# Four mixers and eight gated feed-forward stages on one core: order and form of the last mixer's products, and four smaller edits

## What is computed

```python
# block 1: F0, A, F1, then F2, G, F3       block 2: H, C0, then N, C1
x = x + 0.5 * g * swiglu(modulate(rms_norm(x)), wg, wu, wd)       # F0..F3
x = x + g * mixer(modulate(rms_norm(x)))                         # A, G, H, N
x = x + g * conv_ffn(modulate(rms_norm(x)))                      # C0, C1
# G: z = gelu(h @ w_in); u, v = split(z); v = layer_norm(v)
#    out = (u * (w_s_causal @ v + b_s)) @ w_out
# N: q, k_c, v_c, k_s, v_s, k_w, v_w, gate = split(h @ w_in)       16 heads, 4 groups
#    three softmax branches (compressed, selected, window), each with a sloped
#    distance bias; out = (sigmoid(gate) weighted sum of the branches) @ w_out
```

## Time and profile before

| what | value |
|---|---|
| median of three runs | 1769.36 us (1767.43 to 1771.12) |
| the profiled execution | 1770.44 us, span 1768.8 us |
| mean granted TensorE clock | 0.995 |
| busy share of the span | PE 97%, DVE 80%, ACT 52%, POOL 24% |
| moved by DMA | 411 MB, 233 GB/s |

### The profile page before, as it was taken

The page is one execution under the profiler, slowest core; times in us unless marked ns, Lnnn a source line. Parts: engine busy times, 40 slices in busy tenths (PEclk is TensorE's granted clock), DMA queues, the critical chain, the costliest instruction groups (busy, mean ns, idle before and its releaser), DMA issues. The chain is left out here.

```text
span 1768.8 us, 36564 instructions
## 1 busy us (share of the span) xinstructions
PE 1723.2 (97%) x14077; PEld 1679.1 (95%) x14077; DVE 1419.0 (80%) x1914; ACT 911.9 (52%) x1274; POOL 420.1 (24%) x685
## 2 busy tenths in 40 slices
PE   7999999999999999999999999899999999999998
PEld 6999999999999999989999998889999997799998
DVE  6767898788869878877977899869988996578555
ACT  3443367864345533466543366556444557664444
POOL 5322311013223223120122344421222123401000
PEclk9999999999999999999999999999999999999999
DMA  9998857548987888855698865335989593147550
GB/s 338 358 340 271 301 182 265 168 165 307 325 285 250 282 275 303 287 203 195 232 333 269 303 218 202 108 120 168 329 292 305 154 236 111 48 138 256 170 187 24
DMA packets 261793, 411.45 MB, mean 233 GB/s; under 512 B 21950, under 2 KB 204414, under 8 KB 261560
## 3 DMA queue, kind: packets, MB, share of 16 engines
q1 hardware_dynamic: 224968, 290.67, 50.0%
q0 software_dynamic: 36720, 119.36, 19.1%
HBM read 408.90 MB, written 2.63 MB: 233 GB/s over the span
## 5 line engine op out<-in xcount | busy, mean ns | idle before, releaser
L2786 DVE TENSOR_TENSOR lo<-raw,hi 128x2048 fp32r<-128x2048 f32 (+1 forms) x257 | 581.6, 2265 | 178.8 <-ACT hi L2613 178.5
L2613 ACT CAST hi<-raw 128x2048 fp32r<-128x2048 f32 (+1 forms) x266 | 499.0, 1879 | 385.6 <-PE dacc L2305 194.5
L2303 PE MATMUL up<-operand_hi,hi 128*128 128x256 f32 x1952 | 553.8, 284 | 2.4 <-DVE lo L2786 2.4
L2304 PE MATMUL up<-operand_lo,hi 128*128 128x256 f32 x1952 | 553.1, 283 | 0.0
L2305 PE MATMUL up<-operand_hi,lo 128*128 128x256 f32 x1952 | 553.0, 283 | 0.0
L2082 POOL DMA_DIRECT2D ada<-in_ada_w_dram x448 | 260.0, 597 | 816.8 <-DVE ada_acc L2822 753.4
L2303 PEld LDWEIGHTS up<-operand_hi,hi 128*128 128x128 f32 x1952 | 375.3, 192 | 3.3 <-DVE lo L2786 3.0
L2304 PEld LDWEIGHTS up<-operand_lo,hi 128*128 128x128 f32 x1952 | 375.4, 192 | 0.0
L2305 PEld LDWEIGHTS up<-operand_hi,lo 128*128 128x128 f32 x1952 | 375.4, 192 | 0.0
L2822 DVE SCALAR_TENSOR_TENSOR ada_acc<-ada,c_col,ada_acc 128x512 f32<-128x512 f32 x420 | 318.9, 759 | 13.1
L2303 PE MATMUL dacc<-act_hi,hi 128*128 128x256 f32 x1072 | 303.6, 283 | 2.6 <-DVE act_lo L2999 2.6
(11 more groups left out here) (459 smaller groups left out, 2734.6 us busy)
## 6 DMA issues: line engine op xcount, KB each, us to landing
ada<-in_ada_w_dram POOLq DMA_DIRECT2D x448, 256.0 KB, 4.6
raw<-in_ffn_wg_dram SPq DMA_DIRECT2D x88, 512.0 KB, 5.3
raw<-in_ffn_wu_dram SPq DMA_DIRECT2D x88, 512.0 KB, 5.1
raw<-in_ffn_wd_dram SPq DMA_DIRECT2D x88, 512.0 KB, 5.4
raw<-in_ffn_w_up_dram SPq DMA_DIRECT2D x88, 512.0 KB, 4.5
raw<-in_ffn_w_down_dram SPq DMA_DIRECT2D x46, 512.0 KB, 4.4
raw<-in_hg_w_in_dram SPq DMA_DIRECT2D x32, 512.0 KB, 4.9
raw<-in_attn_w_qkv_dram SPq DMA_DIRECT2D x24, 512.0 KB, 7.7
```

Of the source, the lines that this page charges most:

```text
L2303: pe.matmul(o, stat[0], mov[0], start=start, stop=False, skip_group_check=True)
L2304: pe.matmul(o, stat[0], mov[1], start=False, stop=False, skip_group_check=True)
L2613: last = act.copy(put(slab(hi, s, SPL)), take(slab(raw, s, RAW)))
L2786: last = dve.tensor_tensor(put(slab(lo, s, SPL)), take(slab(raw, s, RAW)), put(slab(hi, s, SPL)).bitcast(F32), ALU.subtract)
```

## The change

1. N, gates: slab b+8 is split over its 48 gate columns only and multiplied with these as stationary operand (24 matmuls of 256 columns, 48 x 256 out); ScalarE copies the rows, two small transposes bring them to positions x 48, then the sigmoid.
2. N, order: the gate transposes and scores(0) stand between the two halves of slab b+9, the turn of the compressed probabilities between the halves of b+10. ScalarE copies these before the second value slab. VectorE scales head 1 ahead of head 2's bias and minimum. GpSimd makes the bias of head n + 2 before it waits for head n's coefficients.
3. N, end: the splits of the output slabs b+11 to b+13 move behind the head loop on VectorE and to its last rounds or behind it on ScalarE (b+11 ahead of the loop); the idle products go; the output's first two banks no longer wait for the last results.
4. Vector 23 is now among F3's five; vector 18 is made in G (tiles between the splits, its sum behind the output). H makes none; its wait for the last left-over vector stands ahead of slab b+9.
5. G: the first value slab waits for each half of the scaled gate products separately, its loops are exchanged, and the first half is scaled ahead of the normed operand; slab b+8's low split is halved around the affine step, b+9's stands later.
6. F0: the first four tiles of vector 2 are loaded with the others behind the first slab's use instead of ahead of the bias table.
7. C0, C1: the first conv's bias step is chained on ScalarE instead of counted.

```diff
-FIRST_VEC = {"F0": 2, "A": 7, "F1": 8, "F2": 13, "F3": 18, "H": 23, "C0": 24, "C1": 29}
+FIRST_VEC = {"F0": 2, "A": 7, "F1": 8, "F2": 13, "G": 18, "F3": 19, "C0": 24, "C1": 29}
...
+            if s == BASE["N"] + 8:
+                gate_cols = lambda t: t.rearrange("p (k n) -> p k n", k=KB)[:, :, SEQ - 3 * NSA_HEADS:SEQ]
+                return [(gate_cols, gate_cols)]
...
             raw_products("G")
-            pe.wait_ge(S["up_scaled"], raw_first.index("G") + 1)
             for m in range(4):
                 slab_ready(b + 2 + m)
-                row_product(b + 2 + m, operand_stat(m), m == 0, m == 3, normed_count("G") - KB + 2 * m + 2)
+                row_product(b + 2 + m, operand_stat(m), m == 0, m == 3, normed_count("G") - KB + 2 * m + 2,
+                            first_of="G" if m == 0 else None)
                 if m == 2:
                     turn_weights()
             for m in range(2):
@@ -999,7 +1003,11 @@
                 if c >= 2:
                     pe.wait_ge(S["gelu_done"], 3 + c)
                 mix(c)
-            pe_out("G", pe, slab_ready, down_product, operand_mov)
+            for m in range(4):
+                slab_ready(b + 8 + m)
+                pe.wait_ge(S["operand_ready"], 4 * OPND["Go"] + m + 1)
+                down_product(b + 8 + m, operand_mov(m), m == 0, m == 3)
+            ada_sum(FIRST_VEC["G"])
...
             for m in (4, 5, 6, 7):
                 split_lo(b + m)
+                for k in {5: (0,), 6: (1,), 7: (2,)}.get(m, ()):
+                    ada_tile(FIRST_VEC["G"], k)
...
-            split_lo(b + 8)
+            split_lo_half(b + 8, 0)
             dve.wait_ge(S["bs_in"], 48)
             affine(0)
             affine(1)
-            split_lo(b + 9)
+            split_lo_half(b + 8, 1)
             gate(0)
             gate(1)
             gated_lo(0)
             gate(2)
             gated_lo(1)
+            split_lo(b + 9)
             gate(3)
             gated_lo(2)
             gated_lo(3)
             for m in (10, 11, 12):
                 split_lo(b + m)
+                for k in {10: (3,), 11: (4, 5), 12: (6, 7)}.get(m, ()):
+                    ada_tile(FIRST_VEC["G"], k)
             residual("G")
...
-                if c == 2:
-                    pe.wait_ge(S["mod_done"], 24)
...
+                if m == 9:
+                    pe.wait_ge(S["mod_done"], left_vector("H") + 1)
...
-            ada_sum(23, o=bank(up, 1))
...
-            ada_tile(23, 0)
-            ada_tile(23, 1)
...
-            ada_tile(23, 2)
...
-                if m < 14:
-                    ada_tile(23, m - 6)
...
             for n in range(NSA_HEADS):
+                if n + 2 < NSA_HEADS:
+                    nsa_pool_bias(pool, n + 2)
                 pool.wait_ge(S["ncoef"], n + 1)
                 early = n_prob[n % 3][:, 512:768].rearrange("p (r k) -> p r k", r=2)
                 c = n_coef[:, 4 * (n % 3):4 * (n % 3) + 2]
                 pool.tensor_tensor(early, early, c.unsqueeze(2).to_broadcast([P, 2, P]),
                                    ALU.mult).then_inc(S["nearly_scaled"], 1)
-                if n + 2 < NSA_HEADS:
-                    nsa_pool_bias(pool, n + 2)
...
+            def gate_columns(m):
+
+                w = 3 * NSA_HEADS
+                slab_ready(b + m)
+                for k in range(KB):
+                    o = (k + 1) * SEQ - w
+                    dst, stat = bank(dacc, 0)[0:w, 0:SEQ], [slab(t, b + m, SPL)[:, o:o + w] for t in (hi, lo)]
+                    pe.matmul(dst, stat[0], op_k(operand_hi, k), start=(k == 0), stop=False, skip_group_check=True)
+                    pe.matmul(dst, stat[0], op_k(operand_lo, k), start=False, stop=False, skip_group_check=True)
+                    last = pe.matmul(dst, stat[1], op_k(operand_hi, k), start=False, stop=(k == KB - 1), skip_group_check=True)
+                last.then_inc(slab_used, 1)
+
+            def turn_gates():
+
+                w = 3 * NSA_HEADS
+                pe.wait_ge(S["ngate_done"], 1)
+                for t in range(NT):
+                    last = pe.transpose(bank(dacc, 0)[:, SEQ + t * w:SEQ + (t + 1) * w], gate_rows[0:w, t * P:(t + 1) * P],
+                                        ident[0:w, 0:w])
+                last.then_inc(S["ngate_pe"], 1)
...
-            tokens(8, bank(dacc, 0), SEQ - 3 * NSA_HEADS, 3 * NSA_HEADS)
-            pe.wait_ge(S["nlo_done"], 6)
-            scores(0)
-            tokens(9, bank(dacc, 3), 0, SEQ)
+            gate_columns(8)
+            def gates_and_scores():
+                turn_gates()
+                pe.wait_ge(S["nlo_done"], 6)
+                scores(0)
+
+            tokens(9, bank(dacc, 3), 0, SEQ, gates_and_scores)
             pe.wait_ge(S["cl_done"], 1)
             scores(1)
-            tokens(10, bank(dacc, 2), 0, SEQ)
-            turn_compressed()
+            tokens(10, bank(dacc, 2), 0, SEQ, turn_compressed)
             for n in range(2, NSA_HEADS + 3):
                 if n < NSA_HEADS:
                     scores(n)
                 if n < NSA_HEADS + 2:
                     turn_probs(n - 2)
-                else:
-                    pe.wait_ge(S["nb_done"], NSA_HEADS)
-                    keep_warm(bank(up, 0), WARM)
                 if n == 3:
                     pe.wait_ge(S["nv_done"], 2)
                 if n >= 3:
                     values(n - 3)
 
-            pe.wait_ge(S["no_done"], NSA_HEADS // 2)
-            pe_out("N", pe, slab_ready, down_product, operand_mov)
+            def out_bank(q):
+
+                if q >= 2:
+                    pe.wait_ge(S["no_done"], NSA_HEADS // 2 - 3 + q)
+
+            for m in range(4):
+                slab_ready(b + 11 + m)
+                pe.wait_ge(S["operand_ready"], 4 * OPND["No"] + m + 1)
+                down_product(b + 11 + m, operand_mov(m), m == 0, m == 3, bank_free=out_bank if m == 0 else None)
...
-            split_hi(b + 10)
             act.wait_ge(S["kc_pe"], 2)
...
-            act.activation(gates, bank(dacc, 0)[:, 0:NT * 3 * NSA_HEADS], ACT.Sigmoid).then_inc(S["ngate_done"], 1)
-            split_hi(b + 11)
+            act.copy(gate_rows[0:3 * NSA_HEADS, :], bank(dacc, 0)[0:3 * NSA_HEADS, 0:SEQ]).then_inc(S["ngate_done"], 1)
+            split_hi(b + 10)
+            act.wait_ge(S["ngate_pe"], 1)
+            act.activation(gates, bank(dacc, 0)[:, SEQ:SEQ + NT * 3 * NSA_HEADS], ACT.Sigmoid).then_inc(S["ngate_done"], 1)
...
             exps(0)
             act.wait_ge(slab_used, b + 10)
             act.copy(vs_sb, bank(dacc, 3)).then_inc(S["nv_done"], 1)
-            split_hi(b + 12)
+            split_hi(b + 11)
             exps(1)
-            act.wait_ge(slab_used, b + 11)
-            act.copy(vw_sb, bank(dacc, 2)).then_inc(S["nv_done"], 1)
-            split_hi(b + 13)
             act.wait_ge(S["npt_pe"], 1)
             for j in range(2):
                 last = act.copy(c_pt[:, j * 512:(j + 1) * 512], bank(dacc, j))
             last.then_inc(S["npt_done"], 1)
+            act.wait_ge(slab_used, b + 11)
+            act.copy(vw_sb, bank(dacc, 2)).then_inc(S["nv_done"], 1)
             for n in range(2, NSA_HEADS + 3):
                 if n < NSA_HEADS + 2:
                     probs_back(n - 2)
                 if n < NSA_HEADS:
                     exps(n)
+                if n == NSA_HEADS + 2:
+                    split_hi(b + 12)
                 if n % 2 == 0 and n >= 4:
                     result(n - 3)
+            split_hi(b + 13)
             split_hi(b + 14)
...
             key_rest(1)
+            split_lo(b + 10)
             for n in range(NSA_HEADS + 1):
+                if n == 2:
+                    scale(1)
                 if n < NSA_HEADS:
                     bias_and_max(n)
                 if n == 0:
-                    split_lo(b + 10)
                     compressed_probs()
-                if n:
+                elif n != 2:
                     scale(n - 1)
-                if n in (0, 1, 3):
-                    split_lo(b + (11, 12, 0, 13)[n])
                 if n >= 8 and n % 4 == 0:
                     operand_rest(n // 4 - 2)
+            split_lo(b + 11)
+            split_lo(b + 12)
             operand_rest(3)
+            split_lo(b + 13)
             split_lo(b + 14)
...
-            for k in range(ATILES):
-                ada_load(pool, FIRST_VEC[phases[0]], k)
...
+                        if p == phases[0]:
+                            pool.wait_ge(slab_used, 1)
+                        for k in range(0 if p == phases[0] else ATILES, KB):
...
+                    for k in range(ATILES, KB):
+                        ada_load(pool, FIRST_VEC[p], k)
...
-                    for kk, t in [(kk, t) for kk in range(2) for t in range(NT)]:
+                    for t, kk in itertools.product(range(NT), range(2)):
+                        if first_of is not None and part == 0 and kk == 0:
```

(21 more changed lines are left out.)

27 lines of the change are left out of this document (11 added, 16 removed).

## The result

The changed kernel takes 1751.25 us (median of 4 runs, 1751.16 to 1752.15) against 1768.61 us (1767.43 to 1771.12): a ratio of 0.9899, interval 0.9887 to 0.9912, so 17.4 us less. The forecast was 1752.0 us. Another series, on another chip, gave 1752.53 us and 0.9908 (0.9895 to 0.9920).

What follows compares the result with a forecast made beforehand. TensorE, busy 97% of the span, was taken as the bound. N 13.6 + H 1.7 + F0 2.6 - G 0.3 = 17.6 us off 1770.44 gives 1752.8; with the median 1.1 lower, forecast 1752.0 us, range 1747 to 1762.

Steps and rivals of the forecast that it cites:

- N, gate slab and clock: N, slab 8 and behind: 24 wide matmuls replace 48 narrow ones, 3.5 us less; no low clock behind, 1.7 less.
- 5.9/48 = 0.123 us per matmul: N, slab 8: a full slab's time per matmul, pricing the 24 new matmuls at 2.95 us, 3.5 us less.
- N, stalls: N, entry to the head loop: waits on the compressed probabilities' copy (2.0) and VectorE's third scaling (1.8) go; 4.0 us.
- N, loop: N, head loop: bias one head ahead makes TensorE the bound; four pairs save 1.0 us, five heads behind as much; 2.0 us.
- N, end: N, end of head loop: eight idle products (1.98 us) and the output slabs' wait for the last result (0.46) go; 2.4 us.
- G: Gating mixer G: takes the modulation vector's tiles; its reordering's gain is lost again as VectorE has no idle time; costs 0.3 us.
- H: Hgrn mixer H: without the vector's tile ahead of the low-part splits, differences and TensorE's wait behind them come 1.7 us earlier.
- F0: Start phase F0: second slab's cast 0.9 us earlier and, as the gap halves, the clock's 1.7 us; 2.6 us.
- (1): N and F0: the clock still falls, giving back 3.4 + 1.7 us: 1757 us; chance 0.15.
- (2): N's tail becomes a wait: one slab late (4.2 us), the loop's 2.0 and F0 gain lost: 1761 us; chance 0.10.
- (3): N's loop turns wait on another engine, stalls only move; no loop, stall or F0 gain: 1760 to 1766 us; chance 0.10.
- (4): N, head loop: clock falls inside it and stays, making the kernel slower; whole loop low gives 1798 us; chance 0.03.

Runs made afterwards that it cites:

- Experiment 1: Changed kernel with slab 8's gate columns multiplied as before (48 matmuls streaming 48 columns, no two small transposes; split still over 384 columns): 1757.18 us.
- experiment 7: Changed kernel with the transposes of the compressed probabilities behind slab 10 again instead of between its halves: 1753.34 us.
- experiment 8: Changed kernel with the splits of output slabs 11 to 13 in the head loop again (ScalarE's casts of 12 and 13 ahead of it): 1755.16 us.
- experiment 2: Changed kernel with GpSimd making the bias of head n+2 behind the early product of head n again: 1753.59 us.
- experiments 3 and 4: Changed kernel with the eight idle products put back, between the value products of heads 14 and 15 (1755.79 us) or behind those of head 15 (1754.23 us).
- all_together: Changed kernel with alternating value products for heads 0 to 11, one G tile earlier, head 3's first scores and N's second hidden group later: 1746.42 us.

## Why the prediction was right

The time (1752.0 against 1751.25 and 1752.53), the sign and the stages were right, some of the terms only in their sum. The last step of the sum is rounded (1752.8 less 1.1 is 1751.7). By the two profiles the gain was 19.3 us where the sum had 17.6; that the medians meet so closely is in part the draw of the clock. The signs named in the forecast came: slab 8 in 2.82 us with no low clock behind it, no wait above 0.3 us ahead of the turns, a pair in 6.64 us, the first level product's wait down to 0.36 us, F0's second slab at 45.60 us.

- **N, gate slab and clock: 3.5 + 1.7 forecast, 5.25 measured.** Slab 8's start to the scores of head 2 took 22.27 us and takes 17.02. The sum is right, the split is not: the step "5.9/48 = 0.123 us per matmul" was good for the wide product, but I set it against 6.5 us that held 1.1 us of low clock. The product gives 2.6 less 0.3 for the transposes (my low end was 2.4), the clock the other 3.0, which is what 6.8 us at 0.213 instead of 0.120 us per product cost. Experiment 1 shows the first and brings back one of the two stretches.
- **N, stalls: 4.0 forecast, 4.26 measured** (scores of head 2 to those of head 6, 16.24 to 11.98 us). The causes were weighed wrongly. I gave the compressed turn's place 2.0 us; it is worth 0.76 (experiment 7). The splits were worth over 3 (experiment 8): VectorE's stand ahead of two scalings, as I had it, and what I missed is that ScalarE's cast and copy of a slab also stood ahead of its copies of the compressed probabilities.
- **N, loop: 2.0 forecast, 1.67 measured** from head 6 to the last pair, 1.74 by experiment 2. A pair at 6.64 and four at 26.54 us are the forecast's numbers (6.64, 26.56). Only "the five heads behind hold about as much" was too high.
- **N, end: 2.4 forecast, 3.26 measured** (1536.64 to 1542.67 before, 1520.61 to 1523.38 after). The term that I missed: the filler had kept two heads apart that run side by side. That is 0.7 to 0.9 us (experiments 3 and 4).
- **G: costs 0.3 forecast, 0.4 measured.** The mechanism was right point by point: the wait moved to the next value slab, the output started 1.5 us earlier relative to G's entry, the residual began at 830.66, which is 833.3 less the 2.6 of F0, and the gain was lost again: 0.9 us on the sums, and 0.9 at F3's entry (0.69 of it counted as a wait).
- **H: 1.7 forecast, 2.6 measured,** of which 1.7 is the wait ahead of the first level product (2.04 to 0.36). Two profiles without low clock in H show it in 165.97 us, and before, without the 1.5 us that its low stretch cost, it would have been 168.0: 2.0 us by the edit. The other 0.6 is where the clock happened to fall: in output slabs before (1.5 us), partly under waits after (0.9).
- **F0: 2.6 forecast, 2.6 measured in that profile, but right by luck.** The step "as the gap halves, the clock's 1.7" failed: the low stretch is there in six of twelve profiles with the short wait, and not in the one with the long wait put back. The edit is worth 0.8 to 1.0.

The rivals: (1), that the clock still falls in N and F0, is refuted for N (none of the twelve profiles with the wide product has it in slab 9) and half true for F0. (2) and (3) did not come: no slab of the tail waited, and ScalarE became the bound only in the version with pairs. (4) did not come at full size; experiment 8 shows that it was not idle talk. The Trainium skill ("TensorE: Matmul & The Clock Gate", Part 4) says that transposes don't count as busy for the clock gate: twelve of the thirteen loops ran wholly at 1.00 with 13 us of transposes in them (16 turns of 0.82), so the traces do not bear it out for this mix. In the thirteenth, experiment 8, the level fell behind waits of 1.4 us.

**Where the other two us of the gain are.** The profiled run before had a mean clock of 0.995, that after 0.998. Of 31 further runs of the kernel before, the ten with a mean clock of 0.997 or more took 1765.2 to 1767.8 us, the 21 at 0.994 to 0.996 took 1768.5 to 1772.1. On one chip alone they lay between 1765.2 and 1771.0 us: two runs of one kernel differ by a third of what the whole change brings. The mean clock goes with the time in these runs; nothing here sets it by hand.

## What to carry to other kernels

Take a low-clock stretch in one profile as one draw: price an edit by the engines' order of time, count the clock only where the same work has it in several runs, and look at the mean clock beside every time. When a wait names a copy, read that engine's whole queue ahead of the copy: the fix may be the order there, not the place of the work that feeds it. An idle product is not free because it is short: see what it separates; and where one stage gives work to another, time both stages, since here 1.9 us were paid for 2.0.

## What the runs showed of the hardware

- **Two products side by side.** Products with 64 stationary columns that write output rows 0 to 63 and those that write rows 64 to 127 overlap when they are neighbours in TensorE's queue: eight plus eight take 2.15 us one head behind the other, where the second head's first product starts 0.71 us after the first head's (1521.94 against 1521.23), and 1.5 us when issued alternately, as long as eight alone. The Trainium skill ("TensorEngine Tiling (Array Packing)", Theoretical Speedup) gives up to 2x for a side of 64 or less, and these sixteen products show all of it. In the kernel before, scores and transposes over the full array stood between any two heads, and the filler between the last two.
- **A narrow product is not a cheap one.** Streaming 48 columns against 128 stationary ones: 0.112 us each; 256 columns: 0.120; 256 columns against 48 stationary ones: 24 in 2.82 us, 0.118. Up to 256 columns it was the number of products that counted, at full clock; at low clock it was 0.213 for 256 columns and for 48 alike.
- **The same program draws different clocks.** The changed kernel and its versions ran N's compressed scores, hidden products and slab 7 (in all_together in another order) at 1.00 throughout in three of thirteen profiles, and with 3.4 or 6.8 us at 0.50 in ten. From the first compressed score product to the scores of head 0 it is 18.1 us without low clock and 19.6 with 3.4 us of it, so it costs 1.5 us there. What decides this was not settled: it falls behind small products or waits in each case, but not each time.
